# Two input units ahead of the attention loop, and one of four convolution tiles as 31 diagonal matmuls

## The chip, the cores and the metric

The kernel runs on one core of one Trainium2 chip. The metric is the device time of one execution in microseconds (us). Before the change three runs gave 1859.74, 1861.06 and 1861.70 us, median 1861.06 us. The engines are called PE (TensorE), DVE (VectorE), ACT (ScalarE), POOL (GpSimd) and SP (SyncE, which issues DMAs here).

## The reference

A trunk of two layers works on 256 latent tokens and 256 context tokens, each 1024 wide, in float32. Each layer is a half-step SwiGLU FFN, a token mixer, and a second half-step FFN. The mixer of layer 0, to which the change belongs, has a convolution branch and an attention branch. Cut to these:

```python
def conv_module(val, gate, w_dw, b_dw, ln_g, ln_b):
    u = val * jax.nn.sigmoid(gate)
    u = lax.conv_general_dilated(u, w_dw[:, None, :], (1,), [(15, 15)], ..., feature_group_count=512) + b_dw
    return jax.nn.silu(layernorm(u, ln_g, ln_b))          # 31 taps per channel, 512 channels

p = softmax(concatenate([s_band, s_ctx, sink], -1))       # 8 heads of 64, 2 key heads
att_l = p_band @ v_band + p_ctx @ v_ctx                   # window of +-128, and all context keys
yl = concatenate([a_l, att_l], -1) @ w_out                # context tokens likewise, without a band
```

The convolution is depthwise: each of the 512 channels is multiplied with its own 31 weights at 31 shifts along the tokens.

## The kernel before

Activations stand transposed, channels on the 128 partitions and the 512 tokens (256 latent, 256 context) along the free axis. A float32 product that needs full precision is made of three matmuls on values split in a high and a low part (`three`, lines 467 to 472). Weights come in units of 1 MB: SP loads a unit into `raw`, ACT rounds it to `w_hi` (line 970), DVE makes the rest `w_lo` (line 1283), and PE uses it. Units share two slots of each buffer. All engines run their own program in order, and semaphores tie them together; `pe.wait_ge(exp_made, j - 1)` holds PE back until the counter has that value.

The input projection of the mixer has seven units, E to E+6. E and E+1 hold value and gate of the convolution tiles 0 and 1, E+2 and E+3 the queries, E+4 keys and values, E+5 and E+6 the convolution tiles 2 and 3. For the first five PE runs a whole unit at a time. Rotary embedding of five tiles (`rotate` on PE, `rope` on DVE, counter `roped`) follows the query and key units. The gate of a convolution tile passes a sigmoid on ACT, and DVE multiplies it with the value into `upad` (`gated_value`, line 1475).

A convolution tile is 31 DVE instructions, one tap each: the tile in `upad`, shifted by the tap, times a weight for each channel, added to `y` (`taps`, lines 1486 and 1489). The 124 taps of four tiles run in a fixed order, tiles 0 and 1 by turns and then 2 and 3 by turns. 30 of them stand ahead of the attention loop and 94 in it; `taps_by(j)` says how many are done by step j.

The attention has 16 items in the order of `ATT`: for each of four pairs of heads, two blocks of 128 queries, and for each block an item of the latent stream (s = 0, 512 keys) and one of the context stream (s = 1, 256 keys). An item passes the engines so:

- PE `score`: two matmuls of 64 rows, one for each head of the pair. For s = 1 the second waits for the first (`s_half`).
- DVE `largest`: mask and largest score; for s = 0 it also copies the scores into `gact`.
- ACT `expo`: exponentials (line 1106) and the sink's (1110), then DVE `denominator`, then ACT `normalise` (1119).
- PE `turn`: transposes of the weights (line 710: eight for s = 0, four for s = 1).
- ACT `turned`: the copy out of PSUM (line 1128).
- PE `values` (line 724), once for each pair of heads and stream, then ACT `att_head` (1133) and DVE `hn_lo` (1559).

The loops of the three engines run in step. In step j, PE has the scores of item j+1, then the transposes of item j-1, and in some steps `values`. ACT has `expo(j)`, `normalise(j-1)`, `turned(j-2)`. DVE has `largest(j)`, `denominator(j-1)` and its taps. `expo(j)` waits for the transposes of item j-2, and the transposes of item j-1 wait for `turned(j-2)`.

Of unit E+5, four of the eight k steps stand ahead of the loop. Its other four and the eight of E+6 are dealt out over steps 0 to 8 by `CONV_AT` (`conv_step`, six matmuls of 512 columns each). The sigmoids of both gates and the multiplications into `upad` stand in steps 3 and 9 (`GATED_AT`). After the loop PE sums the four `y` tiles for the LayerNorm (line 751) and goes on to the output projection.

Of the kernel before, what the change touches and what calls it, by code (L numbers as in the profile page):

```python
# [38 lines left out]
NMOD = (JOBS - 2) * KT  # L39
UNIT = 2048  # L40
# [46 lines left out]
def build(nc, t, out):  # L87
# [3 lines left out]
    with ExitStack() as ctx:  # L91
# [105 lines left out]
        tap_done = sem("tap_done")  # L197
        pad_clear = sem("pad_clear")
# [77 lines left out]
        def block_place(b):  # L276
# [170 lines left out]
        @block.gpsimd  # L447
        def _(pool):
            def vector_rows(i):

                q = i % SLOTS_MOD
                pool.dma_start(mod_raw[:, q, :], t["mod_w"][i]).then_inc(mod_in[q], 16)  # L452

            for i in range(SLOTS_MOD):
                pool.wait_ge(mod_mm, 5 + i // 2)
                vector_rows(i)
            pool.wait_ge(mod_mm, KT)
            pool.dma_start(c_row.rearrange("p s k -> p (s k)"), t["c_rows"].partition_broadcast(P))\
                .then_inc(c_rows_in, 16)
            for i in range(SLOTS_MOD, NMOD):  # L460
                pool.wait_ge(mod_made, KT + i - SLOTS_MOD + 1)
                vector_rows(i)
# [3 lines left out]
        def _(pe):  # L466
# [173 lines left out]
            def two(b, k):  # L640
                return b * KT * P + k * P
# [17 lines left out]

            def conv_step(c, n):  # L660

                k = n if c == 2 else (n + CT) % KT
                u = E + 3 + c
                if n == 0:
                    pe.wait_ge(lo_made, u + 1)
                    pe.wait_ge(unit_evac, E + 4 if c == 2 else u)
                for b in range(2):
                    last = three(ps[:, 2 + b, :], weights(u, two(b, k), two(b, k) + P),
                                 (hn_hi[:, k, :], hn_lo[:, k, :]), n == 0, n == KT - 1)
                if n == KT - 1:  # L670
                    last.then_inc(unit_mm, 1)

            rotate(2)
            rotate(3)
            conv_step(2, 0)
            conv_step(2, 1)
            pe.wait_ge(v_rows, 1)
            for i in range(4):
                last = pe.transpose(ps[:, 5, i * P:(i + 1) * P], gact[:, 0, i * P:(i + 1) * P], ident)
            last.then_inc(v_mm, 1)  # L680
            rotate(4)
            conv_step(2, 2)
            conv_step(2, 3)

            pe.wait_ge(roped, 5)
            pe.wait_ge(v_made, 1)
# [26 lines left out]
            def values(tt, s):  # L714
# [3 lines left out]
                if g >= 1:  # L718
                    pe.wait_ge(mix_made, g)
                else:  # L720
                    pe.wait_ge(unit_evac, E + 5)
# [5 lines left out]

            NJ = len(ATT)
            pe.wait_ge(unit_evac, E + 5)
            score(0, 0)  # L730
            score(0, 1)
            for j in range(NJ + 7):
                between = [(conv_step, a) for a in CONV_AT.get(j, ())]
                if j + 1 < NJ:
                    score(j + 1, 0)
                    if ATT[j + 1][1] == 1 and between:
                        step, a = between.pop(0)
                        step(*a)
                    score(j + 1, 1)
                for step, a in between:  # L740
                    step(*a)
# [7 lines left out]
            for c in range(CT):  # L749
                pe.wait_ge(tap_done, TAPS * (c // 2) + TAPS - 1 + c % 2)  # L750
# [204 lines left out]
        def _(act):  # L955
# [140 lines left out]
            act.activation(v_att[:].rearrange("p a b -> p (a b)"), ps[:, 5, :], ACT.Copy).then_inc(v_made, 1)  # L1096

# [38 lines left out]
            for j in range(NJ + 7):  # L1136
# [134 lines left out]
        def _(dve):  # L1271
# [206 lines left out]
            def taps(a, b):  # L1478

                for n in range(a, b):  # L1480
                    c, i = 2 * (n // TAPS) + n % 2, n % TAPS // 2
                    if n % TAPS == 0:
                        dve.wait_ge(unit_evac, E + 2 if n == 0 else E + 7)
# [3 lines left out]
                    else:  # L1487
                        dve.wait_ge(tap_done, n - 1)
# [34 lines left out]

# [27 lines left out]
            for j in range(NJ + 8):  # L1551
# [365 lines left out]
```

## Time and profile before

| | before |
|---|---|
| median of three runs | 1861.06 us |
| the profiled execution | 1862.07 us |
| its span | 1860.3 us |
| PE busy | 1777.5 us, 96% |
| DVE busy | 1160.4 us, 62% |
| ACT busy | 622.0 us, 33% |
| POOL busy | 68.7 us, 4% |
| mean granted PE clock | 0.973 |

The span runs from the first to the last instruction; the execution has 1.8 us around it. "Busy" is the time in which an engine had an instruction running. PE is the engine that is busy nearly always. In the slices of the page PE stands below 9 tenths in a few places only: three slices of 46.5 us from about 512 to 651 us show 7, 7 and 6 tenths, and their clocks are 9, 8 and 7 tenths. The first two of them, with the slice ahead, are the attention loop. PE is idle there while DVE and ACT are busy, so what these two and the order of the waits cost shows up in the time.

A row of the timeline has start, length, engine, line, operation, "output<-inputs", shape and count; a bracket says how long the engine was idle before it and what ended that. Several like instructions are merged. The length of a merged row runs to the end of its last instruction, which is about 0.1 us (DVE, ACT) or 0.17 us and more (PE) after the next one may start. So steps are taken from start to start.

### The profile page before, as it was taken

Reading aid. Unit: us, or ns where it says so; the run is one execution under the profiler, and the core shown is the slowest. Engines: PE = TensorE matmul, PEld = TensorE weight load, DVE = VectorE, ACT = ScalarE, POOL = GpSimd, SP = SyncE. Lnnn points to the kernel's source line nnn. Section 1 sums busy time; section 2 is a strip of 40 time slices with the busy share of each in tenths; the row PEclk is TensorE's granted clock in tenths of the full one; section 3 lists DMA queues with packets and bytes.
Section 4 is the critical chain, followed back from the end, with each engine's and each line's share of the span. In section 5 each row is a group of like instructions: output and inputs, shape, how many; then the busy total and the mean of one; then the engine's idle time right before and its main releaser. Section 6 shows DMA issues by size and latency. Waiting matters only on the chain.

```text
span 1860.3 us, 23349 instructions
## 1 busy us (share of the span) xinstructions
PE 1777.5 (96%) x9215; PEld 1488.3 (80%) x9215; DVE 1160.4 (62%) x1766; ACT 622.0 (33%) x824; POOL 68.7 (4%) x133
## 2 busy tenths in 40 slices
PE   9999999999776999999999999999999999899997
PEld 5788888878543778888888788888887999899996
DVE  4477667875868557876777577433335436765454
ACT  4322122233564442222222422222224323544342
POOL 0001001100000000100010000000000000000000
PEclk8999999999887999999999999999999999999998
DMA  9365555552110125555656264233122222235543
GB/s 385 132 201 170 191 166 189 183 182 71 42 39 7 68 68 190 180 175 179 199 162 203 68 198 147 91 110 110 61 99 70 89 69 91 91 137 169 193 164 108
DMA packets 49040, 253.36 MB, mean 136 GB/s; under 512 B 5568, under 2 KB 7104, under 8 KB 32576
## 3 DMA queue, kind: packets, MB, share of 16 engines
q1 hardware_dynamic: 30384, 184.10, 28.8%
q0 software_dynamic: 18576, 68.17, 11.7%
q8 instruction: 54, 0.88, 0.2%
q14 instruction: 26, 0.21, 0.0%
HBM read 251.20 MB, written 1.05 MB: 136 GB/s over the span
## 4 chain that ended last, share of the span: by engine, by line
PE 87%; DVE 8%; ACT 3%; issue 1%; DMA 1%; ACTq 0%; SPq 0%; DVEq 0%
PE ps L470 27%; PE ps L472 27%; PE ps L471 27%; DVE y L1489 3%; DVE w_lo L1283 2%; ACT w_hi L970 1%; PE ps L838 1%; PE ps L517 1%; PE ps L867 1%; DVE t_ring L1339 1%; DVE gact L1533 0%; PE ps L864 0%; DVE hn_lo L1346 0%; PE ps L500 0%; DMA out_y<-t_ring 0%
## 5 line engine op out<-in xcount | busy, mean ns | idle before, releaser
L470 PE MATMUL ps<-hn_hi,w_hi 128*128 128x512 f32 (+2 forms) x1784 | 647.7, 363 | 15.0 <-DVE hn_lo L1346 8.4
L471 PE MATMUL ps<-hn_lo,w_hi 128*128 128x512 f32 (+2 forms) x1784 | 640.7, 359 | 0.0
L472 PE MATMUL ps<-hn_hi,w_lo 128*128 128x512 f32 (+2 forms) x1784 | 640.5, 359 | 0.0
L1283 DVE TENSOR_TENSOR w_lo<-raw,w_hi 128x2048 fp32r<-128x2048 f32 (+2 forms) x184 | 376.9, 2049 | 350.3 <-ACT w_hi L970 350.2
L970 ACT ACTIVATE w_hi<-raw 128x2048 fp32r<-128x2048 f32 (+2 forms) x184 | 316.5, 1720 | 733.7 <-PE ps L472 730.6
L470 PEld LDWEIGHTS ps<-hn_hi,w_hi 128*128 128x128 f32 (+1 forms) x1784 | 338.6, 190 | 78.6 <-issue 13.0
L472 PEld LDWEIGHTS ps<-hn_hi,w_lo 128*128 128x128 f32 (+1 forms) x1784 | 338.8, 190 | 50.5 <-issue 0.8
L471 PEld LDWEIGHTS ps<-hn_lo,w_hi 128*128 128x128 f32 (+1 forms) x1784 | 338.9, 190 | 48.5 <-issue 0.5
L470 PE MATMUL ps<-a_hi,w_hi 128*128 128x512 f32 (+1 forms) x704 | 255.4, 363 | 1.7 <-DVE a_lo L1413 1.7
L471 PE MATMUL ps<-a_lo,w_hi 128*128 128x512 f32 (+1 forms) x704 | 255.2, 362 | 0.0
L472 PE MATMUL ps<-a_hi,w_lo 128*128 128x512 f32 (+1 forms) x704 | 255.2, 362 | 0.0
L1387 DVE CUSTOM_DVE_ANT_0 t_ring<-mod_raw,cols 128x1024 f32<-128x1024 f32 x128 | 164.0, 1281 | 1.8
L1387 DVE CUSTOM_DVE_ANT_0 mod_raw<-mod_raw,cols 128x1024 f32<-128x1024 f32 x128 | 163.9, 1280 | 0.0
L470 PEld LDWEIGHTS ps<-a_hi,w_hi 128*128 128x128 f32 x704 | 132.9, 189 | 22.7 <-DVE a_lo L1413 2.1
L471 PEld LDWEIGHTS ps<-a_lo,w_hi 128*128 128x128 f32 x704 | 132.9, 189 | 20.6
L472 PEld LDWEIGHTS ps<-a_hi,w_lo 128*128 128x128 f32 x704 | 132.9, 189 | 20.5
L1302 DVE SCALAR_TENSOR_TENSOR xT<-ps,modT,xT 128x256 f32<-128x256 f32 x136 | 59.9, 479 | 133.1 <-PE ps L472 133.0
L1029 ACT ACTIVATE a_hi<-prod 128x512 f32 (+3 forms) x88 | 50.9, 579 | 212.7 <-DVE prod L1410 212.7
L452 POOL DMA_DIRECT2D mod_raw<-in_mod_w x128 | 68.0, 531 | 1071.3 <-DVE modT L1387 1028.3
L1413 DVE TENSOR_TENSOR a_lo<-prod,a_hi 128x512 fp32r<-128x512 f32 (+1 forms) x88 | 55.1, 626 | 63.6 <-ACT a_hi L1029 63.6
L1489 DVE SCALAR_TENSOR_TENSOR y<-upad,cols,y 128x512 f32<-128x512 f32 x120 | 81.2, 744 | 0.0
L470 PE MATMUL ps<-w_hi,hn_hi 128*128 128x256 f32 x256 | 76.4, 299 | 0.0
(205 smaller groups left out, 1270.6 us busy)
## 6 DMA issues: line engine op xcount, KB each, us to landing
raw<-in_w_up SPq DMA_DIRECT2D x88, 1024.0 KB, 4.9
mod_raw<-in_mod_w POOLq DMA_DIRECT2D x128, 512.0 KB, 3.9
raw<-in_w_downA SPq DMA_DIRECT2D x32, 768.0 KB, 4.2
raw<-in_w_downB SPq DMA_DIRECT2D x32, 640.0 KB, 3.9
raw<-in_w_od_in SPq DMA_DIRECT2D x16, 1024.0 KB, 4.9
mod_raw<-in_mod_first SPq DMA_DIRECT2D x8, 1024.0 KB, 8.1
raw<-in_w_ev_in SPq DMA_DIRECT2D x7, 1024.0 KB, 4.9
raw<-in_w_ev_out SPq DMA_DIRECT2D x4, 1024.0 KB, 4.8
```

Source lines behind the costliest of these rows:

```text
L452: pool.dma_start(mod_raw[:, q, :], t["mod_w"][i]).then_inc(mod_in[q], 16)
L470: pe.matmul(o, lh, rh, start=first, stop=False)
L471: pe.matmul(o, lh, rl, start=False, stop=False)
L472: return pe.matmul(o, ll, rh, start=False, stop=last)
L517: pe.matmul(ps[:, 7, :], t_ring[:, 0, 0:P], t_ring[:, 0, :], start=True, stop=True)
L970: act.activation(w_hi[:, u0 % 2, 0:n], raw[:, u0 % 2, 0:n], ACT.Copy).then_inc(hi_made, 1)
L1029: act.activation(a_hi[:, j + 2 * r, 0:w], prod[:, j, 0:w], ACT.Copy).then_inc(a_hi_made, 1)
L1283: dve.tensor_tensor(w_lo[:, u0 % 2, 0:n], raw[:, u0 % 2, 0:n], w_hi[:, u0 % 2, 0:n], ALU.subtract).then_inc(lo_made, 1)
L1302: last = dve.scalar_tensor_tensor(out=xT[:, d0 + 2 * r, tokens(s)], in0=ps[:, bank(u0, b), tokens(s)], scalar=modT[:, vec, d0 + 2 * r, s:s ...
L1387: last = dve.tensor_tensor_reduce(out=spent, in0=mod_raw[:, q, :], in1=c_row[:, s, :], scale=1.0, scalar=col("mod_b", m * KT + k), op0=ALU ...
L1413: dve.tensor_tensor(a_lo[:, j + 2 * r, 0:w], prod[:, j, 0:w], a_hi[:, j + 2 * r, 0:w], ALU.subtract).then_inc(a_made, 1)
L1489: ins = dve.scalar_tensor_tensor(out=dst, in0=src, scalar=col("conv_w", i * CT + c), in1=dst, op0=ALU.mult, op1=ALU.add)
```

## The change

- PE runs unit E+5 in one piece (the four transposes of v and the last `rotate` stay after its second k step), then the scores of item 0, then unit E+6 in one piece, and then the loop. `CONV_AT`, `GATED_AT` and `conv_step` are gone.
- ACT has both sigmoids and the rounding of the two units that follow (E+7, E+8) ahead of the loop; the first sigmoid waits for `roped` 5.
- DVE has 24 more taps ahead of the loop, both `gated_value` and both `w_lo` units. It has three tiles, 93 taps, in all: 54 ahead of the loop and 39 in steps 0 to 14.
- Tile 3 goes to PE: POOL multiplies the identity with the tap's weights into a 128x128 diagonal matrix, and PE adds diagonal times shifted `upad` to a PSUM bank, two taps in a step. The diagonals lie in `acc`, `sd` and `rstd`, twelve places; from the thirteenth on POOL waits for the tap twelve before it. ACT copies the sum to `y` and adds the bias in step 17.
- A score for s = 0 waits for `max_made` where it waited for `exp_made`; `largest` for s = 0 has a wait for `exp_made` instead. Scores for s = 1 stand in bank 2, not 1.

```diff
-        CONV_AT = {0: ((2, 4), (2, 5)), 1: ((2, 6),), 2: ((2, 7),), 4: ((3, 0),), 5: ((3, 1), (3, 2)),
-                   6: ((3, 3), (3, 4)), 7: ((3, 5), (3, 6)), 8: ((3, 7),)}
-        GATED_AT = {3: 2, 9: 3}
...
+        TAP_ORDER = [(n % 2, n // 2) for n in range(EARLY + 12)]
+        for _n in range(10):
+            TAP_ORDER += [(2, 2 * _n), (0, 21 + _n), (2, 2 * _n + 1), (1, 21 + _n)]
+        TAP_ORDER += [(2, _n) for _n in range(20, CONV_W)]
+        AHEAD_OF_LOOP = EARLY + 24
...
+            return min(TAPS, AHEAD_OF_LOOP + (TAPS - AHEAD_OF_LOOP) * (j + 1) // 15)
+        DIAGS = 12
+        def diag_place(n):
+            q = n % DIAGS
+            return (acc, sd, rstd)[q // 4][:, q % 4 * P:(q % 4 + 1) * P]
+        def turned_taps(j):
+            return range(2 * (j - 1), min(2 * j, CONV_W)) if j >= 1 else range(0)
...
+            pool.wait_ge(rstd_mm, 2)
+            for n in range(CONV_W):
+                if n >= DIAGS:
+                    pool.wait_ge(turned_tap, n - DIAGS + 1)
+                pool.tensor_scalar(diag_place(n), ident, col("conv_w", n * CT + 3), None, ALU.mult).then_inc(diag_ready, 1)
...
-                if h2 == 0 and j >= 2:
+                if h2 == 0 and j == 1:
+                    pe.wait_ge(unit_evac, E + 6)
+                if h2 == 0 and j >= 2 and s == 0:
+                    pe.wait_ge(max_made, j - 1)
+                if h2 == 0 and j >= 2 and s == 1:
                     pe.wait_ge(exp_made, j - 1)
...
+            def conv_turn(n):
+                if n == 0:
+                    pe.wait_ge(unit_evac, E + 7)
+                pe.wait_ge(diag_ready, n + 1)
+                pe.matmul(ps[:, 3, :], diag_place(n), upad[:, 3, :, n:n + LAT], start=(n == 0), stop=(n == CONV_W - 1))\
+                    .then_inc(turned_tap, 1)
...
             score(0, 0)
             score(0, 1)
+            unit(E + 6, 0, 2, KT, TOK, (hn_hi, hn_lo), two)
             for j in range(NJ + 7):
-                between = [(conv_step, a) for a in CONV_AT.get(j, ())]
                 if j + 1 < NJ:
                     score(j + 1, 0)
...
                     score(j + 1, 1)
-                for step, a in between:
-                    step(*a)
+                for n in turned_taps(j):
+                    conv_turn(n)
...
+            act.wait_ge(roped, 5)
+            for c in range(2, 4):
+                act.wait_ge(unit_mm, E + 4 + c)
+                act.activation(t_ring[:, c % 2, :], ps[:, bank(E + 3 + c, 1), :], ACT.Sigmoid).then_inc(gate_made, 1)
+                head_of(E + 5 + c)
...
+                if j == NJ + 1:
+                    act.wait_ge(turned_tap, CONV_W)
+                    act.activation(y[:, 3, :], ps[:, 3, :], ACT.Identity, bias=col("conv_b", 3)).then_inc(conv_made, 1)
...
+            taps(EARLY, EARLY + 12)
+            gated_value(2, t_ring[:, 0, :], bank(E + 5))
+            rest_of(E + 7)
+            taps(EARLY + 12, AHEAD_OF_LOOP)
+            gated_value(3, t_ring[:, 1, :], bank(E + 6))
+            rest_of(E + 8)
```

The order on DVE just ahead of the loop, before. `w_lo` is the rest of unit E+6, `y<-upad` a tap, `gact,att_cols<-ps` the largest score of item 0.

```order
L1509 TENSOR_TENSOR qk<-t_ring,sq 128x256 [waits link_v]
L1283 TENSOR_TENSOR w_lo<-raw,w_hi 128x2048 [waits hi_made]
L1525 TENSOR_SCALAR att_cols<-cols 128x8
L1533 ISA gact,att_cols<-ps,att_mask 128x512 [waits s_mm,link_v]
L1533 ISA att_cols 128x1
```

The same place after the change:

```order
L1530 TENSOR_TENSOR qk<-t_ring,sq 128x256 [waits link_v]
L1304 TENSOR_TENSOR w_lo<-raw,w_hi 128x2048 [waits hi_made]
L1510 SCALAR_TENSOR_TENSOR y<-upad,cols,y 128x512 [waits tap_done] x12
L1496 TENSOR_TENSOR upad<-t_ring,ps 128x2x256 [waits gate_made]
L1304 TENSOR_TENSOR w_lo<-raw,w_hi 128x2048 [waits hi_made]
L1507 TENSOR_SCALAR y<-upad,cols 128x512 [waits unit_evac]
L1510 SCALAR_TENSOR_TENSOR y<-upad,cols,y 128x512 [waits tap_done] x11
L1496 TENSOR_TENSOR upad<-t_ring,ps 128x2x256 [waits gate_made]
L1304 TENSOR_TENSOR w_lo<-raw,w_hi 128x2048 [waits hi_made]
L1551 TENSOR_SCALAR att_cols<-cols 128x8
L1561 ISA gact,att_cols<-ps,att_mask 128x512 [waits s_mm,link_v]
```

Between the last `w_lo` and the first largest score there are now 24 taps, two products into `upad` and two more `w_lo`.

The order on PE in step 6 of the loop, before: the second half of the scores of item 7, a k step of unit E+6, the transposes of item 5, and `values` of the first pair's context stream.

```order
L696 MATMUL ps<-qk 128x256 [waits s_half]
L470 MATMUL ps<-hn_hi,w_hi 128x512
L471 MATMUL ps<-hn_lo,w_hi 128x512
L472 MATMUL ps<-hn_hi,w_lo 128x512
L470 MATMUL ps<-hn_hi,w_hi 128x512
L471 MATMUL ps<-hn_lo,w_hi 128x512
L472 MATMUL ps<-hn_hi,w_lo 128x512
L710 MATMUL ps<-mats,sq 128x128 [waits pT_made,p_made]
L710 MATMUL ps<-mats,sq 128x128 x3
L724 MATMUL ps<-pT_ctx,v_att 64x256 [waits mix_made,pT_made]
```

The same step after the change, and the start of the next:

```order
L706 MATMUL ps<-qk 128x256 [waits s_half]
L743 MATMUL ps<-upad,rstd 128x512 [waits diag_ready] x2
L720 MATMUL ps<-mats,sq 128x128 [waits pT_made,p_made]
L720 MATMUL ps<-mats,sq 128x128 x3
L734 MATMUL ps<-pT_ctx,v_att 64x256 [waits mix_made,pT_made]
L734 MATMUL ps<-pT_ctx,v_att 64x256 x3
L706 MATMUL ps<-qk 128x512 [waits max_made]
L706 MATMUL ps<-qk 128x512
L743 MATMUL ps<-upad,acc 128x512 [waits diag_ready] x2
L720 MATMUL ps<-mats,prod 128x128 [waits pT_made,p_made]
```

Two float32 matmuls of 512 columns stand where up to two k steps stood, and they come in every step from 1 to 15 (one in step 16).

## Rows read from the trace of the kernel before

**Rows 1.** The page, part 4: the chain that ended last, by line.

```profile
PE ps L470 27%; PE ps L472 27%; PE ps L471 27%; DVE y L1489 3%; DVE w_lo L1283 2%; ACT w_hi L970 1%; PE ps L838 1%; PE ps L517 1%; PE ps L867 1%; DVE t_ring L1339 1%; DVE gact L1533 0%; PE ps L864 0%; DVE hn_lo L1346 0%; PE ps L500 0%; DMA out_y<-t_ring 0%
```

**Rows 2.** Stretches: length, busy PE, PEld, DVE, ACT, POOL, clock, DMA.

```profile
520.00:540.00 20.00, 16.73 (x82) 10.43 (x82) 9.80 (x25) 13.68 (x35) 0.00 (x0) 0.99 0.00 0
540.00:560.00 20.00, 11.70 (x46) 5.48 (x42) 19.62 (x39) 11.14 (x24) 0.00 (x0) 0.67 0.32 107
...
620.00:640.00 20.00, 20.00 (x90) 16.54 (x90) 13.11 (x18) 8.87 (x9) 0.00 (x0) 1.00 0.31 106
```

**Rows 3.** Timeline of DVE at the end of the loop.

```profile
578.46 10.02 DVE L1489 SCALAR_TENSOR_TENSOR y<-upad,cols,y 128x512 f32<-128x512 f32 x15
...
592.04 0.41 DVE L1559 TENSOR_TENSOR hn_lo<-ps,hn_hi 128x256 fp32r<-128x256 f32 x1
592.37 4.05 DVE L1489 SCALAR_TENSOR_TENSOR y<-upad,cols,y 128x512 f32<-128x512 f32 x6
```

**Rows 4.** Timeline of PE there: the last LayerNorm sums.

```profile
595.82 1.98 PE L751 MATMUL ps<-y,mats 128*128 128x512 f32 x4 [1.34 <-DVE y L1489]
```

**Rows 5.** Timeline of DVE ahead of the loop, and its gate product.

```profile
472.66 6.71 DVE L1489 SCALAR_TENSOR_TENSOR y<-upad,cols,y 128x512 f32<-128x512 f32 x10
...
480.41 2.28 DVE L1283 TENSOR_TENSOR w_lo<-raw,w_hi 128x2048 fp32r<-128x2048 f32 x1
...
482.81 0.69 DVE L1533 CUSTOM_DVE_ANT_0 gact<-ps,att_mask 128x512 f32<-128x512 f32 x1
...
500.96 0.69 DVE L1475 TENSOR_TENSOR upad<-t_ring,ps 128x512 f32<-128x512 f32 x1 [5.97 <-ACT t_ring L1147]
```

**Rows 6.** Timeline of PE: the first scores.

```profile
480.55 1.99 PE L696 MATMUL ps<-qk 64*128 64x512 f32 x6 [2.73 <-DVE qk L1509]
```

**Rows 7.** Timeline of PE: transposes of items 6, 7, 8.

```profile
529.49 1.04 PE L710 MATMUL ps<-mats,prod 128*128 128x128 f32 x8
...
534.37 0.63 PE L710 MATMUL ps<-mats,sq 128*128 128x128 f32 x4 [1.00 <-ACT pT_full L1128]
...
538.33 1.06 PE L710 MATMUL ps<-mats,prod 128*128 128x128 f32 x8 [2.27 <-ACT pT_ctx L1128]
```

**Rows 8.** Timeline of ACT in the same two steps.

```profile
530.63 0.72 ACT L1106 ACTIVATE prod<-gact,att_cols 128x512 f32<-128x512 f32 x1 [2.56 <-PE ps L710]
...
533.23 1.00 ACT L1128 ACTIVATE pT_full<-ps 128x1024 f32<-128x1024 f32 x1
535.10 0.47 ACT L1106 ACTIVATE sq<-ps,att_cols 128x256 f32<-128x256 f32 x1 [0.87 <-PE ps L710]
...
537.61 0.58 ACT L1128 ACTIVATE pT_ctx<-ps 128x512 f32<-128x512 f32 x1
```

**Rows 9.** Timeline of PE: scores, `values`, and float32 sums of 512 columns.

```profile
487.37 1.13 PE L696 MATMUL ps<-qk 64*128 64x512 f32 x4
...
517.80 1.95 PE L724 MATMUL ps<-pT_full,v_att 128*64 128x256 f32 x16
...
571.58 1.45 PE L696 MATMUL ps<-qk 64*128 64x256 f32 x4
...
603.14 3.78 PE L768 MATMUL ps<-sq,mats 128*128 128x512 f32 x8
606.36 0.80 PE L470 MATMUL ps<-hn_hi,w_hi 128*128 128x512 f32 x1
```

**Rows 10.** Timeline of PE: work after an idle stretch.

```profile
509.49 1.08 PE L710 MATMUL ps<-mats,sq 128*128 128x128 f32 x4 [3.88 <-ACT pT_full L1128]
510.50 2.08 PE L696 MATMUL ps<-qk 64*128 64x512 f32 x4
...
515.66 0.41 PE L471 MATMUL ps<-hn_lo,w_hi 128*128 128x512 f32 x1
```

**Rows 11.** Instructions on `upad`: count, shortest/median/longest in ns, first and last start.

```profile
L1486 DVE TENSOR_SCALAR y<-upad,cols x4: 539/540/548, 452.3 to 541.3; 128x512 f32<-128x512 f32 x4
```

**Rows 12.** Timeline of DVE in the norm ahead of the mixer.

```profile
412.71 0.88 DVE L1346 SCALAR_TENSOR_TENSOR hn_lo<-t_ring,modT,hn_hi 128x256 fp32r<-128x256 f32 x2 [0.19 <-ACT hn_hi L989]
```

More of the change, by code:

```diff
@@ L39 @@
 NMOD = (JOBS - 2) * KT
+MOD_F0 = 54
 UNIT = 2048
@@ L459, in _ @@
                 .then_inc(c_rows_in, 16)
-            for i in range(SLOTS_MOD, NMOD):
+            for i in range(SLOTS_MOD, MOD_F0 + SLOTS_MOD):
+                pool.wait_ge(mod_made, KT + i - SLOTS_MOD + 1)
+                vector_rows(i)
+            pool.wait_ge(mats_in, 16)
+            pool.wait_ge(rstd_mm, 2)
[3 more added lines that the diff above has]
+                pool.tensor_scalar(diag_place(n), ident, col("conv_w", n * CT + 3), None, ALU.mult).then_inc(diag_ready, 1)
+            for i in range(MOD_F0 + SLOTS_MOD, NMOD):
                 pool.wait_ge(mod_made, KT + i - SLOTS_MOD + 1)
@@ L657, in _ @@
             unit(E + 4, 0, 2, KT, TOK, (hn_hi, hn_lo), two)
[L660 to L671, printed above, removed]
             rotate(2)
             rotate(3)
[L675 to L687, printed above, removed]
+            begin(E + 5)
+            for k in range(KT):
+                for b in range(2):
+                    last = three(ps[:, bank(E + 5, b), :], weights(E + 5, two(b, k), two(b, k) + P),
+                                 (hn_hi[:, k, :], hn_lo[:, k, :]), k == 0, k == KT - 1)
+                if k == 1:
+                    pe.wait_ge(v_rows, 1)
+                    for i in range(4):
+                        turned = pe.transpose(ps[:, 5, i * P:(i + 1) * P], gact[:, 0, i * P:(i + 1) * P], ident)
+                    turned.then_inc(v_mm, 1)
+                    rotate(4)
+            last.then_inc(unit_mm, 1)
             def score(j, h2):
                 tt, s, qt = ATT[j]
-                if h2 == 0 and j >= 2:
+                if h2 == 0 and j == 1:
[3 more added lines that the diff above has]
+                if h2 == 0 and j >= 2 and s == 1:
                     pe.wait_ge(exp_made, j - 1)
@@ L726, in values @@
                 last.then_inc(pv_mm, 1)
+            def conv_turn(n):
+                if n == 0:
+                    pe.wait_ge(unit_evac, E + 7)
+                pe.wait_ge(diag_ready, n + 1)
+                pe.matmul(ps[:, 3, :], diag_place(n), upad[:, 3, :, n:n + LAT], start=(n == 0), stop=(n == CONV_W - 1))\
+                    .then_inc(turned_tap, 1)
             NJ = len(ATT)
-            pe.wait_ge(unit_evac, E + 5)
+            pe.wait_ge(roped, 5)
+            pe.wait_ge(v_made, 1)
             score(0, 0)
             score(0, 1)
+            unit(E + 6, 0, 2, KT, TOK, (hn_hi, hn_lo), two)
             for j in range(NJ + 7):
-                between = [(conv_step, a) for a in CONV_AT.get(j, ())]
                 if j + 1 < NJ:
                     score(j + 1, 0)
-                    if ATT[j + 1][1] == 1 and between:
-                        step, a = between.pop(0)
-                        step(*a)
                     score(j + 1, 1)
-                for step, a in between:
-                    step(*a)
+                for n in turned_taps(j):
+                    conv_turn(n)
                 if 1 <= j < NJ + 1:
@@ L1529, in largest @@
                 dve.wait_ge(s_mm, j + 1)
+                if s == 0 and j >= 2:
+                    dve.wait_ge(exp_made, j - 1)
                 top = att_cols[:, 0, 2 * j:2 * j + 2]
```

37 lines of the change are left out of this document (15 added, 22 removed).

## The prediction

> **What bounds the kernel now.** I read the shares of the chain first. The three matmuls of the weight units are 27% each, and the largest entry that is not PE is the convolution tap on DVE, 3% [rows 1], which is some 50 us. So the kernel is a PE kernel with a hole, and the hole is the attention loop. The stretches show who is busy in it. From 520 to 540 PE is busy 16.73 of 20 us at a clock of 0.99 and DVE 9.80. From 540 to 560 DVE is busy 19.62 of 20, PE 11.70 at 0.67 [rows 2]. The second half of the loop is bound by DVE, which has 94 taps in it. It ends with 15 taps in a row and then a few more, the last six from 592.37 to about 596.4 [rows 3], after which PE does its last sums for the LayerNorm and is done at 597.8 [rows 4]. This 597.8 is the mark against which I count: what follows it does the same work before and after.
>
> The first half is bound differently. Transposes of items 6, 7 and 8 start at 529.49, 534.37 and 538.33, with PE idle 1.00 and 2.27 us before the last two [rows 7]. ACT shows why [rows 8]. After the transposes of an s = 0 item it needs 2.60 us from the start of the exponentials to the start of the copy (530.63 to 533.23), 1.00 for the copy, and the next transposes follow at 534.37. That ring is 4.88 us. After an s = 1 item it is 3.96 us (2.51 from 535.10 to 537.61, then 0.58). No engine order makes a pair of items shorter than 8.84 us.
>
> **Ahead of the loop.** On PE the rest of unit E+5 (four k steps of six matmuls, 0.222 us each as 90 of them fill the 20 us from 620 to 640 [rows 2], 5.3 us) fills 2.73 us of waiting for `roped` before 480.55 [rows 6] and ends at about 477.8 + 5.3 = 483.1. Scores of item 0 follow, 1.1 us, and unit E+6, 48 matmuls or 10.7 us, to 494.9. Its `w_lo` is there at 482.6 [rows 5], so it doesn't wait. But DVE is now the late one. From 482.6 it has 12 taps at 0.662 (ten take from 472.66 to 479.28 [rows 5]) 7.9, a gate product 0.6, a `w_lo` 2.2, 12 taps of which one is short 7.7, again 0.6 and 2.2, and a small one 0.2: 21.4 us. `largest(0)` starts at 504.1 where it was 482.81 [rows 5]. Of the two sigmoids and roundings on ACT nothing is on this path: each is ready while DVE is at its taps. The added wait of ACT for `roped` 5 ends at 480.5, before unit E+5 does. PE has only the scores of item 1 after 494.9 and then waits for `largest(0)`, some 9 us, so it starts the loop at half clock.
>
> Then 1.5 us for `largest(0)`, at 505.6 the exponentials of item 0, 1.8, and 2.51 for those of item 1 and normalising item 0 [rows 8]: ready at 510.0. PE meanwhile has the scores of item 2 at half clock, 2.0 (510.50 to 512.5 in rows 10), and two diagonal matmuls. One float32 matmul of 128x512 is 0.805 us at full clock (four between 603.14 and 606.36 [rows 9]), so two are 1.61, or 3.2 at half: 510.9. Transposes of item 0 start at about 511.
>
> **A step of the loop.** PE has, at full clock: transposes 0.97 (s = 0) or 0.55 (s = 1); scores 1.06 (s = 0; rows 9, 1.13 less its tail) or 1.5 (s = 1; 571.58 to 573.09 [rows 9]); two diagonal matmuls 1.61; in six of the steps `values`, 1.9 for sixteen matmuls [rows 9] and half of it, 1.0, for eight. From the transposes of item m to those of m+1 that is:
>
> - m even: 0.97 + 1.5 + 1.61 = 4.1, under the ring of 4.88. For m = 4, 8, 12 with `values` 6.0, above it.
> - m odd: 0.55 + 1.06 + 1.61 = 3.2, under 3.96. For m = 5, 9 with `values` 4.2, above it; m = 13 has no scores, 3.2.
> - m = 14 has no exponentials left: 0.97 + 1.00 and latencies, 2.2.
>
> Sum over m = 0 to 14: 4 x 4.88 + 3 x 6.0 + 5 x 3.96 + 2 x 4.2 + 2.2 = 67.9 us. DVE has 39 taps in 15 steps, 1.7 us a step, with 1.1 for the largest on the mean and 0.3 for a denominator: 3.2 us, hidden. The wait that was added to `largest` (s = 0) is met already, since `denominator` a step before waited for the same count. The loosened score wait I cost at nothing: the PE's idle time before transposes ends with ACT's copy, not with a score [rows 7].
>
> Transposes of item 15 then start at 511 + 67.9 = 578.9. After them: 0.55, `values` 1.9, ACT's and DVE's halves of it about 1.0 (DVE's is 0.41 [rows 3]), `values` 1.0, four sums 3.2. ACT's copy of tile 3 (0.7) lies in this. End 586.5, against 597.8: 11.3 us less at full clock throughout.
>
> **The clock.** PE is busy 4.1 of 4.88 and 3.2 of 3.96 us in a step, 83%. The nearest row is 520 to 540, 84% at 0.99; below it 58% went with 0.67 [rows 2]. After an idle 3.88 us PE ran at half clock from 509.49 to about 515.5, without a pause, before it rose [rows 10]. Such a stretch of 6 us does 3 us of full-clock work, where a step does 83% of its length, so it costs about 6.0 - 3.0/0.83 = 2.4 us. One at the loop's start is partly paid for above. I take one and a half more, 3.7 us.
>
> **POOL.** No row shows a POOL operation with data. The nearest is the DVE one of the same kind, 0.54 us for 512 columns [rows 11], four times as wide. Twelve diagonals are made while PE is at the five units; the other 19 have from 508 to 578, 3.6 us each, before they delay anything. Bounds: 0.1 us (nothing late) and 4 us. I take 0.5, cost 0. The first diagonals are made while DVE does the norm ahead of the mixer, whose first `hn_lo` at 412.71 [rows 12] releases PE. If POOL held DVE up there by one operation, that is 0 to 0.5 us; later tiles have slack, since DVE makes one in 1.7 us and PE uses 2.7. I take 0.
>
> The Trainium skill (SBUF — State Buffer, Who interferes with whom) says that a DVE instruction with two SBUF inputs contends with a GpSimd instruction that reads SBUF, and that one blocks the other fully. A tap is such an instruction, so is `hn_lo`, and each diagonal reads the identity. By that rule two diagonals of 0.5 us a step would lengthen DVE's 3.2 us to 4.2, still under the ring, and the 0.5 us of the norm would be paid; the sum would be 10.8 in place of 11.3. No run before shows it. The skill (GPSIMD Engine Reference, Elementwise — side-by-side cycle accounting) gives 1.8 cycles for an element at best, from which I estimate 0.2 us and a dispatch for 128 columns; no row here shows that either.
>
> **The forecast.** 11.3 less 3.7 is 7.6 us. The profiled execution of 1862.07 would be 1854.5. It stands 1.0 over the median of the three runs, so I predict 1853.5 us. 0.2% of the time, 3.7 us, is about what a measurement of this kernel can tell from none.
>
> **Rivals.**
>
> 1. *The clock holds, and the rings are all there is.* If the s = 1 scores cost 1.1 us (two of 0.43 at full clock and the gap between them) and the clock doesn't fall, `values` steps cost 5.6 and the gain is 12 to 14 us: 1847 to 1849. For it: 84% at 0.99. Against: the loop starts from 9 us of idle PE.
> 2. *PE becomes the bound at half clock, and the kernel is slower or the same.* All of PE's work between the first and last transposes is 4 x 4.1 + 3 x 6.0 + 5 x 3.2 + 2 x 4.2 + 1.8 = 60.6 us at full clock, 121 at half, which is 53 more than 67.9. The gain is gone when 11.3/53 = 21% of the work runs at half clock; at 30% the kernel is 4.6 us slower, 1866. For it: the diagonal matmuls add 25 us of PE work, and between 540 and 560 the clock stood at 0.67 [rows 2]. Against: at half clock PE would be busy all the time, and in the trace that brought the clock back.
> 3. *POOL is the bound.* Over 3.6 us for a diagonal, each further us costs 19 us. At 4.5 us, 17 us more in the loop and the kernel is 6 us slower: 1867. It would take seven times the DVE row for a quarter of its width.
>
> **Chances.** The forecast (4 to 11 us faster) 0.60; rival 1 0.14; rival 2 0.20, half of it within 0.2% and half slower; rival 3 0.06, slower. So faster 0.74, same 0.10, slower 0.16. The range 1846 to 1863 takes in rival 1, the forecast and the better half of rival 2.
>
> **What would show it.** In the changed kernel's profile: `largest(0)` at 504 (give or take 1) after DVE without a gap, and PE idle some 9 us before it. Transposes 4.9 and 4.0 us apart by turns, ended by ACT's copy, except in steps with `values`, where PE has no idle time. Diagonal matmuls 1.6 us for two, never waiting for POOL. DVE idle a quarter of the loop. The last LayerNorm sum at 586 to 591. Wrong it would be if the transposes lay 6 us or more apart (then the clock row tells rival 2), if a diagonal matmul waited for POOL, or if the norm at 412 moved by over 1 us.

## The result and the profile after

| | before | after |
|---|---|---|
| median, five runs each | 1861.06 us (1859.74 to 1864.43) | 1851.05 us (1849.05 to 1853.09) |
| profiled execution: its time, span, mean clock | 1862.07, 1860.3, 0.973 | 1852.6, 1850.8, 0.983 |
| end of the last LayerNorm sum after the loop | 597.8 us | 588.1 us |

The ratio is 0.9945, with a 95% interval of 0.993 to 0.9959: 10.0 us faster, where 7.6 were forecast. The mark moved by 9.7 us and the span by 9.5, so in the profiled executions the gain is all in the stage.

The stretches of the changed kernel (length, busy PE, PEld, DVE, ACT, POOL, clock, DMA), as in [rows 2]:

```profile
495.00:520.00 25.00, 15.21 (x41) 6.15 (x40) 22.74 (x50) 14.86 (x35) 5.06 (x6) 0.73 0.20 79
520.00:540.00 20.00, 18.91 (x86) 9.36 (x87) 12.68 (x35) 13.91 (x38) 8.48 (x9) 1.00 0.01 1
540.00:560.00 20.00, 18.99 (x86) 9.24 (x85) 14.53 (x37) 14.01 (x39) 4.96 (x6) 1.00 0.00 1
560.00:580.00 20.00, 18.24 (x79) 8.51 (x79) 9.87 (x26) 15.63 (x41) 0.00 (x0) 1.00 0.00 1
```

The stretch from 540 to 560, in which DVE had been busy 19.62 us and PE had stood at 0.67, is now one in which PE is busy 18.99 us at 1.00. DVE's rows ahead of the loop (start, us, engine, line) answer to [rows 5]:

```profile
482.37 8.04 DVE L1510 SCALAR_TENSOR_TENSOR y<-upad,cols,y 128x512 f32<-128x512 f32 x12
...
493.59 7.37 DVE L1510 SCALAR_TENSOR_TENSOR y<-upad,cols,y 128x512 f32<-128x512 f32 x11
...
501.47 2.28 DVE L1304 TENSOR_TENSOR w_lo<-raw,w_hi 128x2048 fp32r<-128x2048 f32 x1
...
503.87 0.69 DVE L1561 CUSTOM_DVE_ANT_0 gact<-ps,att_mask 128x512 f32<-128x512 f32 x1
```

The first largest score starts at 503.87, where 504.1 was forecast. PE after its wait for it (the form of [rows 10]), and then a pair of steps with `values`:

```profile
505.43 2.08 PE L706 MATMUL ps<-qk 64*128 64x512 f32 x4 [8.85 <-DVE att_cols L1568]
507.44 3.78 PE L743 MATMUL ps<-upad,acc 128*128 128x512 f32 x4
511.01 1.27 PE L720 MATMUL ps<-mats,prod 128*128 128x128 f32 x8
...
548.26 1.06 PE L720 MATMUL ps<-mats,prod 128*128 128x128 f32 x8 [0.36 <-ACT pT_ctx L1152]
549.26 1.95 PE L734 MATMUL ps<-pT_full,v_att 128*64 128x256 f32 x16
551.13 1.45 PE L706 MATMUL ps<-qk 64*128 64x256 f32 x4
552.51 1.99 PE L743 MATMUL ps<-upad,sd 128*128 128x512 f32 x4
554.34 0.60 PE L720 MATMUL ps<-mats,sq 128*128 128x128 f32 x4
554.87 1.08 PE L734 MATMUL ps<-pT_ctx,v_att 128*64 128x256 f32 x8
555.88 1.13 PE L706 MATMUL ps<-qk 64*128 64x512 f32 x4
556.94 1.99 PE L743 MATMUL ps<-upad,rstd 128*128 128x512 f32 x4
558.77 1.03 PE L720 MATMUL ps<-mats,prod 128*128 128x128 f32 x8
```

From 548.26 on nothing has an idle time in brackets: two steps of 6.08 and 4.43 us, bound by PE. In the steps without `values` the transposes stand 4.88 and 3.96 us apart and wait for ACT's copy. The tail, to [rows 4]:

```profile
579.87 0.63 PE L720 MATMUL ps<-mats,sq 128*128 128x128 f32 x4 [0.34 <-ACT pT_full L1152]
580.43 1.95 PE L734 MATMUL ps<-pT_full,v_att 128*64 128x256 f32 x16
583.41 1.08 PE L734 MATMUL ps<-pT_ctx,v_att 128*64 128x256 f32 x8 [1.04 <-DVE hn_lo L1587]
584.43 3.70 PE L770 MATMUL ps<-y,mats 128*128 128x512 f32 x8
```

The sums now wait for nothing; in [rows 4] they had waited for a tap of DVE.

### The profile page after: what moved, and what is told of

It reads as the page before. It is cut to its first block, busy times and chain, and to the rows that moved or that the text cites. A ratio compares the mean times of both kernels' runs of the same rounds, so it can differ in the third digit from the quotient of the medians.

```text
span 1850.8 us, 23482 instructions
## 1 busy us (share of the span) xinstructions
PE 1788.7 (97%) x9277; PEld 1490.7 (81%) x9277; DVE 1142.1 (62%) x1735; ACT 617.1 (33%) x821; POOL 97.0 (5%) x164
## 4 chain that ended last, share of the span: by engine, by line
PE 88%; DVE 6%; ACT 4%; issue 1%; DMA 1%; ACTq 0%; SPq 0%; DVEq 0%
PE ps L491 27%; PE ps L493 27%; PE ps L492 27%; DVE w_lo L1304 2%; ACT w_hi L989 1%; DVE y L1510 1%; PE ps L857 1%; PE ps L538 1%; PE ps L886 1%; PE ps L743 1%; PE ps L720 1%; PE ps L734 1%; DVE t_ring L1360 1%; PE ps L706 0%; PE ps L546 0%
## 5 line engine op out<-in xcount | busy, mean ns | idle before, releaser
L492 PE MATMUL ps<-w_lo,hn_hi 128*128 128x256 f32 x256 | 72.8, 285 | 0.0
```

The source lines that it names most:

```text
L492: pe.matmul(o, lh, rl, start=False, stop=False)
```

## The experiments

The changed kernel has two parts that could each be the gain: the units are out of the loop, and 31 taps are off DVE. All kernels below were timed in three groups (e1 to e4; e5, e6, e7, e10; e8, e9, e11, e12), each on another chip and beside runs of the kernel before (medians 1861.29, 1860.87 and 1861.68). A median is that of 4 to 11 executions. The mark (end of the last LayerNorm sum) is read from one profiled execution of each; what lies ahead of the stage can shift it by 1 us or so. "The theory" is the forecast's: two rings set the loop, and PE, DVE and POOL fit under them.

**Each part alone.** `e1_units_only` keeps the units ahead of the loop and gives tile 3 back to DVE:

```diff
+        _rest = TAP_ORDER[54:]
+        del TAP_ORDER[54:]
+        for _n in range(39):
+            TAP_ORDER += [_rest[_n]] + ([(3, _n)] if _n < CONV_W else [])
...
-                for n in turned_taps(j):
-                    conv_turn(n)
```

> The changed kernel with tile 3's 31 taps back on DVE (no diagonals, POOL and the copy on ACT gone); the units stay ahead of the loop. Theory A (the gain is the units, the gates and 24 taps out of the loop, and a loop near its rings; the diagonals only keep DVE under the ring): DVE has 70 taps in 15 steps, 4.5 us a step, just at the mean ring of 4.42, and PE is free of 1.8 us a step. The transposes of item 15 come within 3 us of the changed kernel's, total 1849 to 1854. Rival B (the gain is the 20.5 us of DVE work that PE took over): 1860 or more.

`e2_diagonals_only` is the kernel before, with the diagonals put in after unit E+6:

```diff
+            return range(*{10: (0, 5), 11: (5, 10), 12: (10, 15), 13: (15, 19), 14: (19, 23), 15: (23, 27),
+                           16: (27, 31)}.get(j, (0, 0)))
```

> The kernel before with tile 3 as 31 diagonal matmuls on PE (steps 10 to 16, four or five a step, since its gate product comes in step 9) and 63 taps of the other tiles in steps 0 to 14; the two units stay in the loop. Theory A: the first half stays as it was; from step 10 the bound goes from DVE's 6 to 7 us a step to PE's 5 to 7 us. Total 1852 to 1858, less of the gain than the whole change. Rival B (diagonals are the gain): 1850 to 1852, the same as the changed kernel. Rival C (without the units ahead nothing is won): 1861.

Measured: e1 1858.72 us (ratio 0.9988, 0.9979 to 0.9997), e2 1860.26 (0.9996, 0.9987 to 1.0005). So 2.6 us and 1.0 us alone, and 10 together. The value expected for e1 was missed by 5 us. The stretches of e1 say why:

```profile
520.00:540.00 20.00, 14.75 (x58) 8.11 (x58) 16.41 (x40) 13.35 (x36) 0.00 (x0) 0.61 0.00 0
...
560.00:580.00 20.00, 14.19 (x64) 7.56 (x64) 18.58 (x42) 13.56 (x38) 0.00 (x0) 0.74 0.01 1
```

DVE isn't full at 16.41 of 20 us, and PE has a quarter of its time idle; yet the transposes of items 0 to 15 take 74.8 us (511.32 to 586.12) against 68.86 in the changed kernel. The clock is 0.61. PE in e1:

```profile
521.80 1.94 PE L718 MATMUL ps<-mats,prod 128*128 128x128 f32 x8 [1.32 <-ACT pT_ctx L1145]
523.67 2.50 PE L704 MATMUL ps<-qk 64*128 64x256 f32 x4
527.58 1.08 PE L718 MATMUL ps<-mats,sq 128*128 128x128 f32 x4 [1.41 <-ACT pT_full L1145]
528.59 2.08 PE L704 MATMUL ps<-qk 64*128 64x512 f32 x4
```

The transposes take 1.94 and 1.08 us at half clock, 1.06 and 0.63 at full, and they are a link of ACT's ring. The ring is 5.78 us (521.80 to 527.58) in place of 4.88, and 4.41 in place of 3.96: longer by the 0.9 and 0.45 us of the transposes themselves.

Twice more the long ring of e1 comes by way of DVE, with PE's transposes at full clock (542.21, 1.07 us, and 562.67, 1.06 us). The first time, DVE had waited 2.92 us for PE's late scores, then had five taps to do before the next largest score, and so ACT waited for DVE:

```profile
544.29 0.72 ACT L1123 ACTIVATE prod<-gact,att_cols 128x512 f32<-128x512 f32 x1 [1.96 <-DVE att_cols L1558]
...
548.02 1.09 PE L718 MATMUL ps<-mats,sq 128*128 128x128 f32 x4 [3.37 <-ACT pT_full L1145]
```

That interval is 5.81 us, and the two such intervals bring 1.9 of the 5.9 us by which e1's transposes are longer. So in e1 the low clock and the taps given back to DVE both lengthen rings, and the next experiments have to part them.

In e2 the stretch from 540 to 560 still has DVE at 19.79 of 20 us, with two `w_lo` and the taps of the other tiles in it, and the next has PE full:

```profile
540.00:560.00 20.00, 16.69 (x57) 7.47 (x54) 19.79 (x38) 9.09 (x22) 8.48 (x10) 0.89 0.31 106
560.00:580.00 20.00, 19.89 (x80) 9.62 (x79) 11.60 (x27) 10.91 (x29) 7.76 (x10) 1.00 0.00 0
```

With the units in the loop the diagonals can only stand in its last steps, four or five to a step. From 559.30 on PE works without an idle time and its transposes stand 4.3 to 7.8 us apart. So this part alone trades DVE's bound for PE's.

**Is it PE's work that holds the clock?** `e10_units_and_idle_matmuls` is e1 with 31 float32 matmuls at the diagonals' places, the identity times the same window, written to a bank that nobody reads. DVE keeps all 124 taps.

```diff
+                for n in turned_taps(j):
+                    pe.matmul(ps[:, 3, :], ident, upad[:, 3, :, n:n + LAT], start=True, stop=True)
```

> The kernel with the units ahead and all taps on DVE (1858.7 us, PE clock 0.56 to 0.74 in its loop), with 31 matmuls of the same shape, type and place as the diagonal ones put back on PE, times the identity and read by nobody. Theory C (that kernel lacks the gain because PE, with less to do, runs the loop at half clock: transposes of 1.94 in place of 0.97 us lie on the ring): the clock comes back to 1.0, the transposes of item 15 come 3 to 6 us earlier, total 1852 to 1855, faster with more work. Rival D (its 31 more taps on DVE cost the time): 1858 or more, since PE has 27 us more to do and nothing is taken from DVE.

Measured: 1853.60 us (ratio 0.9949, 0.9933 to 0.9966), 5.1 less than e1 with 28 us more work on PE. Its stretch, and two of its transposes:

```profile
520.00:540.00 20.00, 18.63 (x82) 8.69 (x81) 19.72 (x47) 14.78 (x40) 0.00 (x0) 1.00 0.00 1
```

```profile
521.47 1.06 PE L718 MATMUL ps<-mats,prod 128*128 128x128 f32 x8 [0.36 <-ACT pT_ctx L1149]
...
526.37 0.63 PE L718 MATMUL ps<-mats,sq 128*128 128x128 f32 x4 [0.54 <-ACT pT_full L1149]
```

The ring is back at 4.90 us, with all the taps still on DVE (busy 19.72 of 20 us), and from the first to the last transposes it is 69.84 us. So the extra matmuls bring back the full clock, and with it 5.0 of the 5.9 us. By the medians, e1 has 2.6 of the changed kernel's 10.0 us and the idle matmuls add 5.1. The last 2.5 can't be told from nothing: e10 and the changed kernel have ratios of 0.9949 and 0.9945 with intervals that overlap, and their runs scatter by 7 and 4 us. The marks part it better. They are 597.8 us before, 596.3 in e1, 589.5 in e10 and 588.1 in the changed kernel: 1.5 us for the place of the units, 6.8 for the clock and 1.4 for a DVE that is relieved. Most of the last is in the first interval, 6.07 us for 5.11, where ACT waits for a largest score that stands behind five taps:

```profile
513.77 0.72 ACT L1127 ACTIVATE prod<-gact,att_cols 128x512 f32<-128x512 f32 x1 [2.38 <-DVE att_cols L1562]
```

**What was costed at nothing.** `e8_old_score_wait` puts the old score wait back; `e9_pool_twice` makes each diagonal twice.

```diff
-                if h2 == 0 and j >= 2 and s == 0:
-                    pe.wait_ge(max_made, j - 1)
-                if h2 == 0 and j >= 2 and s == 1:
+                if h2 == 0 and j >= 2:
                     pe.wait_ge(exp_made, j - 1)
```

> The changed kernel with the old score wait: scores of item j wait for the exponentials of item j-2 for both streams. Theory: nothing, 1851 us within 0.2%, transposes(0) to transposes(15) 68.9 us as in the changed kernel, because the even transposes' idle time ends with ACT's copy, not with a score. Rival (the loosened wait is a part of the gain): the scores of the full stream start some 1.5 us later in every second step and pass it on to the transposes, 8 steps, 1856 us or more.

```diff
+                pool.tensor_scalar(diag_place(n), ident, col("conv_w", n * CT + 3), None, ALU.mult).then_inc(diag_once, 1)
+                pool.wait_ge(diag_once, n + 1)
                 pool.tensor_scalar(diag_place(n), ident, col("conv_w", n * CT + 3), None, ALU.mult).then_inc(diag_ready, 1)
```

> The changed kernel with each diagonal made twice by POOL, the second after the first, so that each costs 1.5 to 3 us. Theory (POOL has 3.6 us for a diagonal in the loop): 1851 us within 0.2%, and PE still never waits for POOL. Contention rival: twice as many POOL reads of the scratch memory beside the taps lengthen DVE's 3 taps from 2.1 us, but DVE is idle a quarter of the loop, so still under 2 us more. POOL-bound rival: over 3.6 us for a pair of operations in the loop, diagonal matmuls wait for it, 1855 us or more.

Measured: e8 1852.56 us (0.9949, 0.9937 to 0.9962), transposes 511.92 to 580.56, 68.64 us; e9 1850.61 (0.9942, 0.9930 to 0.9954), 510.44 to 579.08, 68.64 too. In the loop both costs are nothing. Ahead of it the old score wait is not quite free: the scores of item 2 start at 507.32 for 505.43, the transposes of item 0 at 511.92 for 511.01, and the mark is 588.8 for 588.1, less than the medians can tell. A pair of POOL operations in e9 takes up to 2.5 us, under the 3.6 us that a diagonal may take:

```profile
514.01 1.74 POOL L481 TENSOR_SCALAR acc<-mats,cols 128x128 f32<-128x128 f32 x1 [1.91 <-PE ps L746]
515.85 0.68 POOL L483 TENSOR_SCALAR acc<-mats,cols 128x128 f32<-128x128 f32 x1
```

**What bounds the changed kernel.** Three edits, each to one term of the forecast's sum: `e3_start_early` moves ten taps and a `w_lo` from ahead of the loop into it, `e4_spread` takes diagonals out of the steps with `values`, `e6_act_order` lets ACT normalise item j-1 and copy item j-2 before the exponentials of item j.

```diff
-        AHEAD_OF_LOOP = EARLY + 24
+        AHEAD_OF_LOOP = EARLY + 14
...
+                if j == 2:
+                    rest_of(E + 8)
```

> The changed kernel with 10 of the 24 taps ahead of the loop moved into it, and the w_lo of unit E+8 into step 2. Theory A (the stage is serial: what DVE does ahead of the loop is paid in full, what it does in the loop is hidden under the ring): the first largest score starts at 496.7 in place of 503.9, total 7 us less than the changed kernel, 1844. Rival B (DVE is near its limit in the loop, so that 10 taps and a w_lo, 8.8 us, come back there): no change, 1851.

```diff
+            count = (0, 2, 2, 2, 3, 2, 1, 2, 3, 2, 1, 2, 2, 2, 1, 2, 2)
+            return range(sum(count[:j]), sum(count[:j + 1])) if j < len(count) else range(0)
```

> The changed kernel with the diagonal matmuls dealt out otherwise: one in place of two in the three steps in which they follow the long `values`, three in steps 4 and 8, two in step 16. Theory A (steps with `values` are bound by PE, the others by the ring): three intervals of 6.07 us become 5.16, two of 4.88 become 5.08, 0.5 more at the end: 1.8 us less than the changed kernel. Rival B (PE's work is the bound in every step): 0.

```diff
-                if j < NJ:
-                    expo(j)
                 if 1 <= j < NJ + 1:
                     normalise(j - 1)
                 if 2 <= j < NJ + 2:
                     turned(j - 2)
+                if j < NJ:
+                    expo(j)
```

> The changed kernel with ACT's step in another order: normalise(j-1), turned(j-2), expo(j), in place of expo(j) first. Theory A (where there are no `values`, the bound is the ring from the transposes of one item over exponentials, normalising and the copy to the next transposes, not PE's work): the copy no longer waits for the exponentials, the intervals of 4.88 and 3.96 go down to PE's work, 4.2 and 3.45, or to ACT's own 3.9 and 3.4: 5 us less than the changed kernel, 1846. Rival (ACT then waits for DVE's denominator in every step, 0.5 us and more, and DVE's taps stand ahead of it): 0 or slower.

| kernel | median (us) | ratio to before, 95% | transposes of items 0 and 15 |
|---|---|---|---|
| changed | 1851.05 | 0.9945 (0.993 to 0.9959) | 511.01, 579.87 |
| e3 | 1845.43 | 0.9922 (0.9908 to 0.9935) | 503.60, 574.74 |
| e4 | 1848.48 | 0.9937 (0.9923 to 0.9950) | 511.32, 578.79 |
| e6 | 1845.12 | 0.9907 (0.9893 to 0.9921) | 511.21, 575.08 |

By the marks, 583.0, 587.0 and 583.3 us, the three edits bring 5.1, 1.1 and 4.8 us on the changed kernel; by the medians 5.6, 2.6 and 5.9, where 7, 1.8 and 5 were expected. In e4 the three long intervals fall from 6.07 to 5.22 us, but 0.2 us of each comes back in the next one, where PE's `values` wait for DVE.

e6: the ring is gone, and PE is the bound at 19.78 of 20 us, with 63.87 us of transposes in place of 68.86. A pair of items without `values` takes 7.6 us (515.61 to 523.20), under the 8.84 us that the prediction held to be the floor for any engine order.

```profile
520.00:540.00 20.00, 19.78 (x86) 9.85 (x86) 14.99 (x38) 16.22 (x43) 6.86 (x9) 1.00 0.00 0
```

e3 starts the loop 7.4 us earlier but gives 2.3 back, because PE falls to half clock behind an idle time of 2.38 us. In the second step its scores take 2.49 us and two diagonals 3.61, and the next transposes come after 7.4 us, where the ring is 4.88:

```profile
503.60 1.60 PE L720 MATMUL ps<-mats,prod 128*128 128x128 f32 x8 [2.38 <-ACT prod L1143]
505.13 2.49 PE L706 MATMUL ps<-qk 64*128 64x256 f32 x4
507.55 3.61 PE L743 MATMUL ps<-upad,acc 128*128 128x512 f32 x4
511.00 0.60 PE L720 MATMUL ps<-mats,sq 128*128 128x128 f32 x4
```

**Together.** `e5_early_spread` is e3 with counts (0, 4, 2, 2, 2, 2, 1, 2, 2, 2, 1, 2, 2, 2, 1, 2, 2), four diagonals where PE was idle; `e7_all_three` is that with ACT's new order.

> The early start (10 taps and a w_lo moved into the loop) with the diagonal matmuls dealt out again: four in step 1, where PE was idle 2.38 us before the first transposes and then ran 7 us at half clock, one in the steps that follow the long `values`. Theory A and C: the first interval goes from 7.4 to 5 us, three others from 6.07 to 5.2: 4 us less than with the early start alone, 1841. Rival: four diagonals push the first transposes back by 2 to 3 us at half clock, so that only 2 us are won, 1843.5.

> Early start, diagonals dealt out again, and ACT's new order together. If the three limits (start, `values` steps, ring) are independent, their gains add up: 6, 3 and 5 us, 1837 to 1838. Rival: with the ring gone PE's work of about 63 us is the bound everywhere, and where the diagonals stand no longer matters, 1840.

Measured: e5 1842.90 us (0.9893, 0.9876 to 0.9910), e7 1840.65 (0.9887, 0.9872 to 0.9903). In e5 the first interval is back at 4.88 us, but the four diagonals ahead of it take 4.52 us, a part of them at half clock (3.71 us in e11 at full), and the first transposes start at 504.89 where e3 has 503.60. By the medians the gains don't add: ACT's order is worth 6 us alone and 2.3 on top of e5. By the marks (580.0 in e5, 578.5 in e7) the three are worth 9.6 us together and 11.0 one by one, so the loss in adding them is between 1.4 and 3.7 us, and it is not well measured. Two new waits show in e7. ACT waits for DVE, which has 3.3 taps a step and the `w_lo`, and PE's `values` wait for it too:

```profile
506.05 0.91 ACT L1144 ACTIVATE sq<-sq,att_cols 128x256 f32<-128x256 f32 x2 [1.05 <-DVE att_cols L1576]
...
511.44 1.33 ACT L1144 ACTIVATE prod<-prod,att_cols 128x512 f32<-128x512 f32 x2 [1.79 <-DVE att_cols L1576]
```

```profile
499.35 1.84 PE L707 MATMUL ps<-qk 64*128 64x512 f32 x4 [1.65 <-DVE att_cols L1568]
501.12 4.64 PE L744 MATMUL ps<-upad,acc 128*128 128x512 f32 x8
...
528.50 1.08 PE L735 MATMUL ps<-pT_ctx,v_att 128*64 128x256 f32 x8 [0.91 <-DVE hn_lo L1587]
```

Two last edits go for these waits: `e11_late_w_lo` moves the `w_lo` to step 15, `e12_idle_pair` puts two idle matmuls where PE was idle 1.65 us.

```diff
-                if j == 2:
+                if j == 15:
                     rest_of(E + 8)
```

> The kernel with all three changes (early start, spread diagonals, ACT order), with the last w_lo of the loop moved from step 2 to step 15, where DVE is idle. Theory: ACT's waits for the denominators in the first steps (1.05, 1.79, 1.26 us) came from that w_lo; without it the first three pairs of steps run at PE's 8.4 us and the kernel gains about 1 us on the 1840.65 us of all three, 1839.5. Rival: the raw slot comes free 60 us later, the load that follows it is late for its unit after the loop, and the kernel loses 2 us or more.

```diff
+                if j == 0:
+                    for n in range(2):
+                        pe.matmul(ps[:, 3, :], ident, upad[:, 2, :, n:n + LAT], start=True, stop=True)
```

> The kernel with all three changes and two more float32 matmuls (128x128x512, identity times the third conv input, read by nobody) between the scores of items 1 and 2, where PE was idle 1.65 us before it ran at half clock. Theory: the clock stays up, scores of item 2 take 1.1 in place of 1.84 us and the four diagonals 3.7 in place of 4.64, less 0.2 us for the matmuls beyond the idle time: transposes(0) 1.5 us earlier, 1839.2 us in place of 1840.65. Rival (the stretch is bound by DVE and ACT, not by the clock): no change.

Measured, four runs each: e11 1841.19 us (1837.54 to 1843.54), e12 1840.70 (1839.39 to 1844.61). Neither can be told from e7. The profiled execution of e11 is the fastest of its four, that of e12 the slowest. In e12 the matmuls did what they were for (first rows), and then PE fell to half clock one pair of steps later, behind a wait of 1.81 us that comes from DVE's `w_lo` by way of ACT:

```profile
496.28 1.99 PE L759 MATMUL ps<-upad,mats 128*128 128x512 f32 x4
498.20 1.13 PE L707 MATMUL ps<-qk 64*128 64x512 f32 x4
...
512.41 1.06 PE L721 MATMUL ps<-mats,prod 128*128 128x128 f32 x8 [1.81 <-ACT pT_ctx L1156]
513.60 2.10 PE L707 MATMUL ps<-qk 64*128 64x256 f32 x4
515.63 3.78 PE L744 MATMUL ps<-upad,rstd 128*128 128x512 f32 x4
```

In e11 the same scores, behind the same 1.65 us of idle time as in e7, ran at full clock in the profiled execution (1.13 us for 1.84, and transposes of item 0 at 502.69 for 505.61):

```profile
498.09 1.13 PE L707 MATMUL ps<-qk 64*128 64x512 f32 x4 [1.65 <-DVE att_cols L1568]
```

Of these 2.9 us, 1.26 were there before the scores, and 1.7 are the clock's. In e3 the same scores behind 1.65 us ran at full clock too (1.13 us), in e5 at half (1.97 us). That is some 2 us between executions of nearly the same program, and enough to hide an edit worth one. I can't say whether e11 and e12 bring something of their own. The fastest version is e7, level with these two, 20 us under the kernel before and 10 under the changed one.

## Why the prediction was right, point by point

- **DVE ahead of the loop, 21.4 us; the first transposes at 511:** right, 503.87 and 511.01. PE's idle time was 8.85 us for 9, and the half clock behind it is in that row.
- **The loop, 67.9 us:** 68.86. The rings were 4.89 and 3.96 us, as read from the rows of ACT before [rows 8]. The diagonal matmul was mis-sized: two take 1.83 us in the loop (552.51 to 554.34), not 1.61. The sums from which I took 0.805 us take 3.13 us for four in the changed kernel (584.43 to 587.56). The rows don't tell why a diagonal takes more. Under the rings that costs nothing. "No engine order makes a pair of items shorter than 8.84 us" was wrong, as e6 shows; it holds for ACT's present order only. The two odd steps that `values` bind took 4.43 us for 4.2, the three even ones 6.07 for 6.0 (there the scores, 1.38 for 1.5, gave most of it back), the first step 5.11 for 4.88 and the last 2.27 for 2.2: together 1.0 us.
- **The tail, 7.6 us:** 8.26 (579.87 to 588.13). The idle 1.04 us for DVE's `hn_lo` was in the sum; the four sums end after 3.70 us for 3.2.
- **The clock, 3.7 us:** this is the term that failed (as a product, one and a half times 2.4, it is 3.6). The half clock of the start ended within the first transposes (1.27 us for 1.03), and from there the loop ran at 1.00 throughout. That is 0.2 us, and it is in the 1.0 above. 11.3 less 1.0 less 0.6 is 9.7, which is what the mark shows, with nothing left for a second fall. Its direction was also misread. I asked how much the clock would take from the gain, and took the diagonals for a load that it might punish. Matmuls in their places are what holds it: with none, in e1, the rings are 5.78 and 4.41 us, and in e10 they are back at 4.90 and 3.96.
- **Rival 1** (the clock holds, 1847 to 1849) had the clock right, but expected shorter `values` steps of 5.6 us, which are 6.08. **Rival 2** (PE bound at half clock) fell: in the rows half clock began only behind idle time of PE, in the changed kernel, e1, e3, e5, e7 and e12, and never under PE's steady work. **Rival 3** (POOL) fell with e9.
- **POOL, 0.5 us:** a diagonal takes 0.60 us alone. In the changed kernel, alone and beside taps (first POOL, then DVE):

```profile
518.96 0.60 POOL L480 TENSOR_SCALAR sd<-mats,cols 128x128 f32<-128x128 f32 x1 [1.62 <-PE ps L743]
519.82 1.51 POOL L480 TENSOR_SCALAR sd<-mats,cols 128x128 f32<-128x128 f32 x1 [0.26 <-PE ps L743]
```

```profile
519.54 2.09 DVE L1510 SCALAR_TENSOR_TENSOR y<-upad,cols,y 128x512 f32<-128x512 f32 x3
```

The tap has a median of 746 ns over its 90 instructions, 744 before, and 864 at most (the tap at 539.74, where a diagonal had begun at 539.69). So in this kernel POOL pays for the meeting, by a factor of 2.5, and DVE nearly nothing. In the norm ahead of the mixer the two `hn_lo` of [rows 12] took 1.08 us for 0.88, and the 0.2 us is inside the bound of 0 to 0.5. The Trainium skill (SBUF — State Buffer, Who interferes with whom) says that a DVE instruction with two SBUF inputs contends with a POOL instruction that reads SBUF. The trace agrees that the two slow each other. The prediction's full block it doesn't show: the slow diagonal that began at 519.82 was done at 521.33, before the three taps were (521.63). My estimate of 0.2 us, dispatch not counted, from the Trainium skill (GPSIMD Engine Reference, Elementwise — side-by-side cycle accounting) is a third of the 0.60 us in the row. Nor was "4.2, still under the ring" right for both rings: it is under 4.88 us and over 3.96.
- **The loosened score wait, nothing:** nothing in the loop, and 0.9 us ahead of it in the profile of e8.

The forecast of the time was 2.5 us too high, and that it came so near is in part luck: the loop and the tail were set 1.6 us too short, and the clock term took off 3.7 us that were never lost. For the largest part of the gain its reason was incomplete: it had DVE's relief and the rings, and not that PE's transposes are a link of the ring and need the full clock to keep it at 4.88 us.

## What to carry to other kernels

When a loop is a ring through several engines and PE is one of its links, read the granted clock before the busy shares: here PE's links took nearly twice as long where it had idle gaps, and work moved onto PE shortened the ring. Price a moved operation also by what it does to the clock, and test that with work that nobody reads, as e10 does. And change the parts one by one: here two parts worth 2.6 and 1.0 us alone were worth 10 together. Where parts are worth a few us and medians scatter as much, read a mark in the profile beside them: three edits worth 14.1 us one by one and 10.4 together by the medians were worth 11.0 and 9.6 by the marks.

## What the runs showed of the hardware

- PE with 14.75 of 20 us busy and idle gaps of 1.3 and 1.4 us in every pair of steps was granted 0.61; with 18.63 busy and gaps of 0.36 and 0.54 it was granted 1.00 (e1 and e10, same stretch).
- An idle time of 1.65 us ahead of the same instructions was followed by half clock in e5 and e7 and by full clock in e3 and e11. The fall is not fixed by the gap alone.
- A POOL `tensor_scalar` of 128x128 float32 takes 0.60 us alone and up to 1.74 beside DVE's taps, whose median stays at 0.75 (0.86 at most).
